# Heads, merge and out stage in one block, wider staging in the expansion, diagonal transposes and a quartered modulation in the set-up

## The reference

```python
h = rmsnorm(x, g_mix) * (1.0 + sc1) + sh1            # sh1, sc1, ... = silu(c) @ w_mod + b_mod
pq, pkv, pkr, hq, hf_f, hf_b, hi, hg, ga, gb = split_cols(h @ w_in)
q  = rmsnorm(pq, g_q) @ w_uq                         # 8 heads of 64 + 32 (rotary)
kv = concat([rmsnorm(pkv, g_kv), ckv_ctx]) @ w_ukv   # 8 heads of 64 keys and 64 values
o_mla = softmax(q k^T * scale) v
o_hg  = hgrn2_branch(hq, hf_f, hf_b, hi, hg, ...)    # gated linear recurrence, both directions
mix = sigmoid(ga) * (o_mla @ w_mla_o) + sigmoid(gb) * (o_hg @ w_hg_o)
x   = x + gt1 * (mix @ w_out)
x   = x + gt2 * conv_glu(rmsnorm(x, g_ffn) * (1.0 + sc2) + sh2)
```

## Time and profile before

| what | value |
|---|---|
| time, median of three runs | 2144.15 us |
| time of the profiled execution | 2142.61 us |
| its span | 2140.8 us |
| granted clock of TensorE, mean | 0.988 |
| PE, DVE, ACT, POOL busy | 97, 44, 30, 36% |
| moved by DMA | 185 MB, 86 GB/s |

### The profile page before, as it was taken

The page is one execution under the profiler, slowest core; times in us unless marked ns, Lnnn a source line. Parts: engine busy times, 40 slices in busy tenths (PEclk is TensorE's granted clock), DMA queues, the critical chain, the costliest instruction groups (busy, mean ns, idle before and its releaser), DMA issues. The chain is left out here.

```text
span 2140.8 us, 28026 instructions
## 1 busy us (share of the span) xinstructions
PE 2072.6 (97%) x11524; PEld 1927.2 (90%) x11524; DVE 948.8 (44%) x1386; ACT 649.6 (30%) x949; POOL 769.9 (36%) x512
## 2 busy tenths in 40 slices
PE   5999999999999989999989899999999999999998
PEld 4889999999999968888789778999999999999996
DVE  5326252525143047566545185245244333533466
ACT  4322323232223254766723211311111121112122
POOL 1143434444132234455526422432332232233290
PEclk9999999999999999999999999999999999999999
DMA  8753111112212284323375332211111111112132
GB/s 288 238 150 33 55 33 55 31 57 60 67 50 58 87 224 132 89 72 96 99 159 193 119 118 72 67 40 50 40 44 46 30 52 48 40 40 79 50 102 96
DMA packets 192961, 185.01 MB, mean 86 GB/s; under 512 B 55193, under 2 KB 159346, under 8 KB 192834
## 3 DMA queue, kind: packets, MB, share of 16 engines
q1 hardware_dynamic: 191538, 178.49, 28.3%
q0 software_dynamic: 1296, 4.72, 0.6%
HBM read 142.41 MB, written 40.78 MB: 86 GB/s over the span
## 5 line engine op out<-in xcount | busy, mean ns | idle before, releaser
L129 POOL TENSOR_TENSOR s_w_lo<-s_w_raw,s_w_hi 128x1024 fp32r<-128x1024 f32 x85 | 219.8, 2586 | 512.0 <-ACT s_w_hi L124 512.0
L2606 PE MATMUL s_ps<-h_hi,s_w_hi 128*128 128x384 f32 x1056 | 353.1, 334 | 0.7 <-ACT gate_pad L2438 0.7
L2606 PE MATMUL s_ps<-h_hi,s_w_lo 128*128 128x384 f32 x1056 | 352.9, 334 | 0.0
L2606 PE MATMUL s_ps<-h_lo,s_w_hi 128*128 128x384 f32 x1056 | 352.8, 334 | 0.0
L662 PE MATMUL s_psum<-h_hi,s_w_hi 128*128 128x384 f32 x984 | 332.9, 344 | 7.4 <-DVE h_lo L1330 7.4
L662 PE MATMUL s_psum<-h_lo,s_w_hi 128*128 128x384 f32 x984 | 325.7, 336 | 0.0
L662 PE MATMUL s_psum<-h_hi,s_w_lo 128*128 128x384 f32 x984 | 325.3, 336 | 0.0
L2606 PEld LDWEIGHTS s_ps<-h_hi,s_w_hi 128*128 128x128 f32 x1056 | 198.2, 188 | 1.5 <-issue 1.0
L662 PEld LDWEIGHTS s_psum<-h_hi,s_w_hi 128*128 128x128 f32 x984 | 185.5, 189 | 15.1 <-issue 12.1
L2606 PEld LDWEIGHTS s_ps<-h_lo,s_w_hi 128*128 128x128 f32 x1056 | 198.2, 188 | 0.4
L2606 PEld LDWEIGHTS s_ps<-h_hi,s_w_lo 128*128 128x128 f32 x1056 | 198.2, 188 | 0.0
(11 more groups left out here) (371 smaller groups left out, 3809.2 us busy)
## 6 DMA issues: line engine op xcount, KB each, us to landing
s_w_raw<-in_w_ffn_in SPq DMA_DIRECT2D x44, 512.0 KB, 3.9
s_w_raw<-in_w_in SPq DMA_DIRECT2D x41, 512.0 KB, 4.1
s_w_mod<-in_w_mod SPq DMA_DIRECT2D x8, 2048.0 KB, 8.1
w_raw<-in_w_ffn_out SPq DMA_DIRECT2D x11, 1024.0 KB
scratch_gates<-sig SPq DMA_DIRECT2D x48, 192.0 KB, 1.9
merge_gates<-scratch_gates SPq DMA_DIRECT2D x16, 576.0 KB, 4.3
scratch_o_mla<-o_raw SPq DMA_DIRECT2D x8, 576.0 KB, 5.0
scratch_x<-x SPq DMA_DIRECT2D x9, 512.0 KB, 2.6
```

Of the source, the lines that this page charges most:

```text
L129: pool.tensor_tensor(flat[0], flat[1], flat[2], ALU.subtract).then_inc(self.lo_ready, 1)
L2606: mm = pe.matmul(ps[bank][:, 0:CH], a[s][:, k, :], b[:, k, j * CH:(j + 1) * CH], start=n == 0, stop=n == 3 * KD - 1)
```

## The change

Three things change at once.

- *Set-up.* DVE no longer scales the tile; it scales the 128x128 identity by the row factors (`scaling`, three buffers), and PE multiplies the tile by that diagonal, so that scaling and transposing are one fp32 product. ACT takes three of the eighteen PSUM banks to `x_t` (`TAKEN_BY_ACT`), DVE the others. The modulation goes in quarters of 256 columns over the whole depth, so that a first quarter serves the depth blocks 0 and 1; its transfers come in pieces of 1 KB where there were pieces of 2 KB. Quarter 0 and the first two chunks of `w_in` are loaded ahead of the other quarters. The exponential of the decay bounds and its table load move behind the splits; the table of the root is loaded by a dummy ahead of the first square.
- *Expansion.* Keys get two pairs of staging tiles and values five; the second key pair lies where `uq_raw` was, the two further value pairs in tiles of the second head's queries.
- *One block.* Heads, merge and out stage become functions that return five lists; the lists of the three stages stand one behind the other in one block, with one set of semaphores and one PSUM tensor. In place of the barriers stand waits on semaphores of the stage before. The barrier between stage_project and the heads stays.

```diff
+TAKEN_BY_ACT = (5, 11, 17)
@@ stage_project, SP
-                load_piece(0)
-                load_piece(1)
+                load_piece(0)
                 load(0)
                 load(1)
-                load_piece(2)
-                load_piece(3)
+                for i in range(1, QUARTERS):
+                    load_piece(i)
@@ stage_project, PE
-                            last = pe.transpose(psum[:, n % 6, x * P:(x + 1) * P], x_rows[t][:, f * P:(f + 1) * P], cst.ident[:, :])
+                            last = pe.matmul(psum[:, n % 6, x * P:(x + 1) * P], x_rows[t][:, f * P:(f + 1) * P],
+                                             scaling[t % 3][:, :], start=True, stop=True)
...
                 for k in range(KD):
+                    if k + 1 < QUARTERS:
+                        piece_product(k + 1)
                     first_chunks(k)
-                    if k < 2:
-                        piece_product(2 + k)
-                    if k == 2:
-                        piece_columns(1)
@@ first_chunks, between its two chunks
+                        if c == 0 and k + 1 < QUARTERS:
+                            piece_columns(k + 1)
@@ stage_project, ACT
                 for t in range(TILES):
                     x_square(t)
-                split(0)
-                take_piece(0)
+                    if t == TILES - 2:
+                        take_piece(0)
+                    if 2 * t - 3 in TAKEN_BY_ACT:
+                        x_take(2 * t - 3)
+                split(0)
+                x_take(2 * TILES - 1)
                 split(1)
@@ stage_project, DVE
-                    dve.tensor_scalar(x_rows[t][:, :], x_rows[t][:, :], rstat[:, 2, t:t + 1], None, ALU.mult).then_inc(xs_ready, 1)
+                    if t >= 3:
+                        dve.wait_ge(xt_ps, 2 * (t - 2))
+                    dve.tensor_scalar(scaling[t % 3][:, :], cst.ident[:, :], rstat[:, 2, t:t + 1], None, ALU.mult).then_inc(xs_ready, 1)
@@ stage_attention, ACT (and DVE alike)
-                        if x > 0 and u == 0:
-                            act.wait_ge(k_stored, 32 * x)
+                if x == 1 and u == 0:
+                    act.wait_ge(uq_lo_ready, 2)
+                if x >= 2 and u == 0:
+                    act.wait_ge(k_stored[x % 2], 32 * (x // 2))
...
-                        if x >= 3:
-                            act.wait_ge(v_stored[x % 3], 32 * (x // 3))
+                if x >= V_RING:
+                    act.wait_ge(v_stored[x % V_RING], 32 * (x // V_RING))
@@ stage_merge, SP
+        load_w(2)
+        load_w(3)
+        for i in range(2):
+            sp.wait_ge(att["o_stored"][i], 16 * HEADS // 2)
+        sp.wait_ge(att["den_stored"], 16 * (HEADS - 1))
+        sp.wait_ge(att["x_lo"], KB)
                 at = (HEADS - 1) * P
                 sp.dma_start(home.den9[:, :], ...)
-                load_w(2)
                 load_x(KB)
                 load_x(KB + 1)
-                load_w(3)
@@ stage_merge, PE
+        pe.wait_ge(att["x_lo"], KB)
                 for c in range(CHUNKS_M):
                     if c >= 2:
                         pe.wait_ge(w_lo_ready, c - 1)
+            else:
+                pe.wait_ge(att["w_lo"], c + 1)
+            if c == 1:
+                pe.wait_ge(att["o_read"], 2 * HEADS)
@@ stage_out_ffn, SP
+        sp.wait_ge(merge["quotient"], KD // 2)
                 load_wo(4)
                 load_wo(5)
+        sp.wait_ge(merge["bank"], 6 * KD)
+        sp.wait_ge(merge["gated"], 6 * KD)
+        sp.wait_ge(merge["m_lo"], KD)
@@ stage_out_ffn, PE
+        pe.wait_ge(merge["wo_lo"], WO_HERE)
                 for k in range(KD):
                     if k >= WO_HERE:
                         pe.wait_ge(wo_lo_ready, k - WO_HERE + 1)
+            pe.wait_ge(merge["m_lo"], k + 1)
                     for o in range(6):
+                if k == 0 and o in (0, 5):
+                    pe.wait_ge(merge["gated"], 6 * KD - 3 + o // 5)
@@ program
-    stage_attention(nc, io, cst, lower, more, low, up, home)
-    stage_merge(nc, io, cst, home, m_hi, m_lo, partial)
-    stage_out_ffn(nc, io, cst, base, m_hi, m_lo, h2_hi, h2_lo, home)
+    with ExitStack() as ctx:
+        sems = Signals(nc, ctx, "s4")
+        psum = ctx.enter_context(nc.psum_tensor("late_psum", [P, 8, 512], F32))
...
+        with nc.Block() as block:
+            @block.tensor
+            def _(pe):
+                att_tensor(pe)
+                merge_tensor(pe)
+                out_tensor(pe)
```

More of the change, by code:

```diff
@@ L419, in block_totals, with takes @@
     return [v[:, :, h].unsqueeze(2).to_broadcast([P, n, b]) for h in range(2)]
-HALF_MOD = KD // 2
+QUARTERS = 4
+QW = D // QUARTERS
+QK = KD // QUARTERS
+TAKEN_BY_ACT = (5, 11, 17)
+def takes(n):
+    act = sum(x <= n for x in TAKEN_BY_ACT)
+    return ("act", act) if n in TAKEN_BY_ACT else ("dve", n + 1 - act)
 def stage_project(nc, io, cst, base, upper, h_hi, h_lo, low, up):
@@ L441, in stage_project @@
         x_t = first("x_t", [P, KD, NT])
-        pieces = piece_a + [first(f"w_mod_b{i}", [P, 4, D]) for i in range(2)]
-        m_rows = [first(f"m_rows{i}", [P, 2, 512]) for i in range(2)]
+        pieces = piece_a + [first(f"w_mod_b{i}", [P, KD, 2 * QW]) for i in range(2)]
+        m_rows = [first(f"m_rows{i}", [P, 2, QW]) for i in range(2)]
         first_end = first.at
@@ L465, in stage_project @@
         ostat = early("ostat", [P, 2 * TILES])
+        lbt = early("lbt", [P, 24])
         assert early.at <= low.sig_at - 2 * NT * 4 - KD * 32 * 4
@@ L548, in columns, with x_taken, x_t_done @@
             return C_HG + (dict(H_STREAMS)[kind] * HH + n) * P
+        def x_taken(engine, n):
+            by, count = takes(n)
+            engine.wait_ge(xt_act if by == "act" else xt_dve, count)
+        def x_t_done(engine):
+            engine.wait_ge(xt_dve, 2 * TILES - len(TAKEN_BY_ACT))
+            engine.wait_ge(xt_act, len(TAKEN_BY_ACT))
         def places(k, dst):
@@ L1411 @@
 B_RING = 6
+V_RING = 5
 B_SHIFT = -len(B_UNITS) % B_RING
@@ L2862, in program @@
     home = MergeHome(nc, base + half, upper, low.end)
-    stage_attention(nc, io, cst, lower, more, low, up, home)
-    assert lower.at <= upper and more.at <= HIGH
     mix = Arena(nc, base)
```

2472 lines of the change are left out of this document (1259 added, 1213 removed).

## The result

The changed kernel takes 2128.02 us (median of 4 runs, 2126.49 to 2130.82) where the kernel before, beside it, takes 2144.07 (2143.12 to 2145.16): a ratio of 0.9929, 95% interval 0.9917 to 0.9941, 16 us faster. The forecast was 2118.7, its range 2111 to 2127. The sign was right; the size was not, and the median lies 1 us outside the range.

A forecast was written before the change was run, and what follows sets the result against it. TensorE, 97% busy of 2140.8 us, was taken as the bound, leaving its idle time and half clock to win. 6.7 + 6.0 + 3.7 + 9.0 = 25.4 took the median from 2144.15 to 2118.7, range 2111 to 2127.

The forecast's parts named there:

- The set-up: 6.7 forecast: Set-up: first product 3.5 us earlier, clock 2.2, two later waits 2.1, less 1.1 for columns; bounds 12 and -4.
- from the start of the affine step to the first product it took 40.54 - 36.68 = 3.86: Set-up: this earlier duration was reused to put the first product at 37.0, 3.5 us earlier.
- TensorE now idles only some 2.5 us ahead of the first product, so I take this as won: Set-up: the half clock behind the first product, costing 2.2 us, was counted as gone.
- The rival that the clock falls again: Remaining waits in set-up, expansion and merge bring back half clock: 2.2 + 2.4 + 2.1 = 6.7 us, 2125.4; chance 0.18.
- The forecast's -4 as a low bound: Set-up: low bound of the gain, in us, if all nine tiles ran at half clock.
- The slower rival: Set-up: diagonal products keep TensorE at half clock to the end of the first chunks, 2167 us; chance 0.03.
- The expansion: 6.0 forecast: Expansion: ScalarE goes on 3.6 us earlier and 2.4 of half clock is won; bounds 8 and 2.
- with two key pairs the store waited for is some 30 us old. ScalarE goes on 3.6 earlier: Expansion: ScalarE's key-store wait goes; TensorE idles 2.1 us and not 5.7.
- The rival that the wider staging does not do what it says: Expansion: the store queue is the limit and the 6.0 us only move to the heads' loads, 2124.7; chance 0.09.
- The 2.4 of the clock: Expansion: half of 4.76 us of half-clock work, won if TensorE's idle time is too short for the clock to fall.
- Heads to merge: 3.7 forecast: Border from heads to merge: 7.5 us for barrier and clock, less 3.8 waiting in chunks 5 and 6; bounds 7.5 and 1.6.
- Merge to out stage: 9.0 forecast: Border from merge to out stage: 6.8 us of wait and 2.2 of clock won; bounds 9.0 and 6.

The follow-up runs named there:

- run 7: Changed kernel, ScalarE splitting the first weights a tile earlier, VectorE making the second chunk's low half instead of GpSimd; first chunks end 63.39 us from the first transpose.
- run 2: Changed kernel plus 30 unread products of 256 columns on TensorE in the gap before the first chunks; that stretch took 31.9 us, 36.0 in the changed kernel.
- run 3: Changed kernel with the values' scratch laid out so that stores write 2 KB pieces; the expansion takes 82.99 us instead of 88.86.
- run 5: Changed kernel with the merge's loads of the last four heads' rows moved two chunks later, behind weights; the merge takes 105.98 us, 2.5 more.
- run 6: Changed kernel with the first four heads' rows loaded ahead of the last head's output store; the merge takes 100.17 us, 103.53 in the changed kernel.
- run 1: Changed kernel with GpSimd's second set-up weight split held until the affine step is done; first product 33.92 us from the first transpose, 34.38 in the changed kernel.

## Why the prediction was right in sign and wrong in size

**The set-up: 6.7 forecast, nothing won in the profiled execution.** The working held to 0.6 us up to `gain_mix`; two steps behind it did not.

The first is "from the start of the affine step to the first product it took 40.54 - 36.68 = 3.86". The 3.86 were copied from a place where nothing collided, and why nothing did stood in the trace of before, in rows the prediction did not read:

```profile
34.07 2.34 POOL L129 TENSOR_TENSOR s_w_lo<-s_w_raw,s_w_hi 128x1024 fp32r<-128x1024 f32 x1 [1.39 <-ACT s_w_hi L124]
...
35.63 0.80 DVE L1314 TENSOR_SCALAR gain_mix<-mod 128x8 f32<-128x8 f32 x1
```

GpSimd's split ended at 36.41, `gain_mix` was held until 36.43, and only then came the affine step. Counted from the first transpose, the change moves VectorE's chain to `gain_mix` 3.3 us earlier and the two splits 1.2 and 0.6 later, so the chain runs into both. `gain_mix` takes 1.35 more (1.51 against 0.16 in run 7). Without that the affine step would wait for ScalarE's copy of the last bank, which ended at 32.23, and start at 27.5 from the first transpose, as it does in run 7, and not at 28.4: 0.9 lost. The affine step itself takes 2.04 more. Together 2.9 of the 3.5 that were to be won, and 2.9 is what run 7 wins back. The other 0.6 went ahead of the collision: the copy of the last bank came at 27.5 where the forecast had 33.1 - 6.23 = 26.9. The Trainium skill ("SBUF — State Buffer", SBUF: two separate sides) says that VectorE and GpSimd share one pair of ports as an exclusive lock: a GpSimd instruction, or one of VectorE in a 2-port mode or with two inputs from SBUF, takes it for its whole length, and the other is blocked. The traces agree: 1.51 and 4.09 beside a split, 0.16 and 2.05 away from it, and 0.22 for `mod`, whose other input lies in PSUM, beside it; the second split, which the affine step was ahead of, took 2.91 where 2.35 is usual. It was the rule to weigh, and it was not weighed.

The second is "TensorE now idles only some 2.5 us ahead of the first product, so I take this as won". With the collision it idled 4.11, behind 1.52 shortly before, and the half clock lasted ten microseconds. The forecast counted 2.2 won; run 2 shows 4.1 lost against a full clock, and runs 3 and 5, with the same set-up as the changed kernel, 1.4 and 1.3. The rival that the clock falls again had this mechanism at 2.1 to 2.4 in each of three places; it came true in one, at nearly double the price in this execution. The waits left in the expansion and the merge lowered no clock in this trace. In runs 2 and 7, whose merge is the same, the wait in chunk 6 (1.80 and 2.17) did, and the merge took 104.3 and 104.9; in run 7:

```profile
1115.00:1119.00 4.00, 3.69 (x13) 3.69 (x14) 2.48 (x4) 1.75 (x2) 1.54 (x2) 0.57 1.05 375
```

The forecast's -4 as a low bound had the clock in it but not the neighbour. The rest of the step held: the columns in quarters, the 1 KB pieces in time for the chunks (348 GB/s in the first line below, between the 290 and 387 of the earlier trace rows), the stretch of 31.9 at full clock. The slower rival, diagonal products holding the clock down, did not come: the window 14 to 17, all of it diagonal products, reads 1.00 (second line):

```profile
32.00:34.00 2.00, 0.89 (x9) 0.29 (x13) 1.93 (x4) 1.17 (x2) 1.10 (x2) 1.00 1.09 348
...
14.00:17.00 3.00, 3.00 (x29) 3.00 (x28) 2.62 (x8) 2.52 (x6) 0.00 (x0) 1.00 1.03 393
```

**The expansion: 6.0 forecast, 2.5 measured, 3.0 without what the barrier's clock does.** The failed step is "with two key pairs the store waited for is some 30 us old. ScalarE goes on 3.6 earlier". The store was, and ScalarE did, for one unit; then it stood 2.59 and 5.27 at the stores of the queries, which wait in the same queue. The rival that the wider staging does not do what it says named this cause and had a chance of 0.09; its own row was the 230 GB/s at a share of 1.05 in the earlier trace rows, full engines at 230 where 2 KB pieces came at 387. More staging buys depth there and not rate. The 2.4 of the clock did come: behind the old stall TensorE's 4.76 us of work ran at half clock, and in none of the six traces with the changed expansion did the clock fall there. So of the 3.0 only 0.6 are left for the stall, where 3.6 were forecast: the waits for `att_tops` went from 6.2 to 5.0 in sum; they were cut up more than shortened. The Trainium skill ("DMA: Bandwidth & Descriptors", Specifications) puts the smallest transfer at line rate at 512 bytes, and the values went out in 256: the traces agree, 228 against 310 GB/s for the same window. The prediction weighed this rule for the modulation and not for the values, where it spoke against the change.

**Heads to merge: 3.7 forecast, 3.8 measured.** The barrier and its clock came off, together 7.2; the two waits for weights in chunks 3 and 6 cost 3.4 (103.53 against 100.17 in run 6; forecast 3.8, in chunks 5 and 6). That the rows in the queue are what delays the weights is shown by run 6.

**Merge to out stage: 9.0 forecast, 9.05 at the first `h_y`.** Then 2.05 were lost again at something the change does not touch. The waits for the next `h_y` are the same in both kernels (2.36 and 0.56 before, 2.40 and 0.56 after). Before, the clock behind it stayed at 1.00, with 20 products in four microseconds; before and after:

```profile
1262.00:1266.00 4.00, 4.00 (x20) 3.32 (x21) 3.97 (x3) 0.97 (x1) 2.39 (x1) 1.00 0.05 15
...
1246.00:1250.00 4.00, 4.00 (x13) 3.12 (x12) 3.97 (x3) 0.50 (x1) 2.37 (x1) 0.57 0.00 0
```

It stayed up in run 6 too, and the rest of the span is 1.6 shorter there than in the changed kernel (941.70 against 943.29 from the out stage's first product). The other half microsecond is not explained. Why the clock falls at this wait in eight of the eleven traces and not in three stays open.

So 5.6 of the 11 us that are missing in the profile lie in the set-up, 3.5 in the expansion and 2.0 behind the out stage's border. The range was too narrow for two of its terms to fail at once, of which one had a low bound of 2 and the other one of -4.

## What to carry to other kernels

A duration taken from the trace holds only for the neighbours that the instruction had there: before a chain is moved earlier, lay the other engines' timelines beside its new place, GpSimd's against VectorE's above all. When an engine waits for a store, look at the size of the pieces and at the GB/s of the full queue before adding buffers: here the size alone was worth 7.6 us, the buffers alone 3.0, and beside the size nothing. What a removed wait gives is worth what the granted clock does behind the next one, so look at that window as well.

## What the runs showed of the hardware

- One instruction of VectorE with four elements per partition took 1.51 us beside a GpSimd split and 0.16 without it; it ended with the split. GpSimd is held in its turn: a split that started 0.1 us behind an affine instruction of VectorE took 2.91, else 2.35. The same subtraction of 128x1024 (`s_w_lo`) took 2.35 on GpSimd and 1.22 on VectorE.
- The same wait costs differently from run to run, by where the clock falls and rises. Ahead of the first chunks, four runs of one set-up (the changed kernel, runs 3, 5 and 6; gaps of 4.11 to 5.7) took 36.0, 33.3, 33.2 and 36.1 us for the stretch behind it, which takes 31.9 at full clock; behind 2.86 us it did not fall, in two runs out of two. Nor does the length of the wait decide: in chunk 6 of the merge the clock fell behind 1.80 and 2.17 us (runs 2 and 7) and not behind 1.84, 1.76 and 1.90 (the changed kernel, runs 1 and 3). Behind the barrier ahead of the heads the half clock cost 1.4 to 3.1 us, in eleven traces of the same instructions. A single execution says nothing of differences that small until this is taken out of it.
- Pieces of 1 KB arrived at 348 GB/s, of 512 bytes at 290, of 2 KB at 387; stretches in which most packets had 256 bytes moved 230 and 225 GB/s with the engines full (799 to 806, before and after).
